# Routing order read out between the halves of the shared block, a gather in parts, and three weight loads that change places

## The reference

```python
def moe_ffn(h, w_router, router_bias, w_gate_up, w_down, shared_gate_up, shared_down):
    xf = h.reshape(-1, D)
    scores = jax.nn.sigmoid(xf @ w_router)
    sel = scores + router_bias
    grp = sel.reshape(N, N_GROUPS, N_EXPERTS // N_GROUPS)
    gscore = jnp.sum(lax.top_k(grp, 2)[0], axis=-1)
    _, gidx = lax.top_k(gscore, TOPK_GROUPS)
    ...
    _, idx = lax.top_k(jnp.where(emask, sel, -jnp.inf), TOP_K)
    w = jnp.take_along_axis(scores, idx, axis=1)
    w = w / jnp.sum(w, axis=-1, keepdims=True) * ROUTED_SCALE
    routed = routed_experts(xf, idx, w, w_gate_up, w_down)
    shared = swiglu(xf, shared_gate_up, shared_down)
    return routed + shared

def swiglu(x, w_gu, w_dn):
    g, u = jnp.split(x @ w_gu, 2, axis=-1)
    return (jax.nn.silu(g) * u) @ w_dn
```

## Time and profile before

| | us |
|---|---|
| median of 3 runs | 1260.34 |
| lowest, highest | 1259.62, 1261.03 |
| the profiled execution | 1259.55 |
| its span in the trace | 1257.70 |
| PE busy | 1081.1 (86%) |
| DVE busy | 505.1 (40%) |
| ACT busy | 248.6 (20%) |
| HBM read | 500.04 MB, 398 GB/s over the span |

### The profile page before, as it was taken

One profiled execution on the slowest core, in us unless ns is written; L12 is line 12 of the kernel. 1 busy time (PEld: TensorE's weight loads), 2 busy tenths in 40 slices (PEclk: granted clock), 3 DMA queues, 4 the chain that ended last, 5 costly groups with the idle time before them and its releaser, 6 DMA issues.

```text
span 1257.7 us, 16869 instructions
## 1 busy us (share of the span) xinstructions
PE 1081.1 (86%) x6524; PEld 599.6 (48%) x6524; DVE 505.1 (40%) x1131; ACT 248.6 (20%) x575; POOL 0.4 (0%) x5
## 2 busy tenths in 40 slices
PE   8999999998787868687879999999778687968786
PEld 6887586544333334343326678655333333424332
DVE  3597975432313132223236887542322313222322
ACT  1031722111101010101023472221100101110101
POOL 0000000000000000000000000000000000000000
PEclk9999999998889888899899999999988988989998
DMA  9999998999999999999999927899999999999996
GB/s 346 393 410 412 407 364 361 414 424 430 425 427 429 425 424 429 423 428 426 424 415 397 405 99 276 355 411 422 429 426 427 427 427 425 430 423 429 424 424 280
DMA packets 86327, 502.22 MB, mean 399 GB/s; under 512 B 9545, under 2 KB 34022, under 8 KB 43494
## 3 DMA queue, kind: packets, MB, share of 16 engines
q1 hardware_dynamic: 85782, 500.91, 97.0%
q10 hardware_dynamic: 464, 0.20, 0.1%
HBM read 500.04 MB, written 1.05 MB: 398 GB/s over the span
## 4 chain that ended last, share of the span: by engine, by line
PE 48%; DMA 39%; DVE 6%; SPq 5%; issue 2%; ACT 0%; DVEq 0%
PE bank L810 40%; DMA w_gu<-in_moe_w_gate_up 24%; DMA xn_hT<-in_moe_w_gate_up 10%; PE bank L813 2%; SPq L628 2%; DMA w_dn<-in_moe_w_gate_up 2%; PE bank L1087 2%; DMA w_gu_x<-in_ada_w 2%; SPq L635 1%; PE bank L1296 1%; PE bank L937 1%; PE bank L1135 1%; DMA ring<-in_ada_w 1%; DVE ada_row L2084 1%; DVE s_sb L1841 1%
## 5 line engine op out<-in xcount | busy, mean ns | idle before, releaser
L810 PE MATMUL bank<-w_gu,ring 128*32 128x512 f32 (+1 forms) x1408 | 350.3, 661 | 109.5 <-DMA xn_hT<-in_moe_w_gate_up 57.0
L810 PEld LDWEIGHTS bank<-w_gu,ring 128*32 128x32 f32 (+1 forms) x1408 | 97.3, 130 | 294.0 <-issue 293.5
L1995 DVE TENSOR_TENSOR hh<-sg,bank 128x256 f32<-128x256 f32 x44 | 27.3, 621 | 402.1 <-ACT sg L1581 402.1
L810 PE MATMUL bank<-w_gu_x,ring 128*32 128x512 f32 (+1 forms) x320 | 162.4, 664 | 9.7 <-DMA w_gu<-in_moe_w_gate_up 9.7
L810 PE MATMUL bank<-xn_hT,ring 128*32 128x512 f32 (+1 forms) x304 | 129.4, 586 | 17.8 <-DMA w_gu<-in_moe_w_gate_up 17.8
L810 PE MATMUL bank<-w_dn,ring 128*32 128x512 f32 x208 | 106.8, 733 | 14.8 <-DMA w_gu<-in_moe_w_gate_up 14.8
L1581 ACT ACTIVATE sg<-bank 128x256 f32<-128x256 f32 x44 | 16.9, 384 | 483.4 <-PE bank L810 483.4
L2012 DVE SCALAR_TENSOR_TENSOR bank<-bank,w_slot,gate 128x512 f32<-128x512 f32 x88 | 66.6, 759 | 89.3 <-PE bank L810 89.1
L810 PE MATMUL bank<-sel,h_hi 128*128 128x256 f32 x352 | 87.8, 290 | 0.0
L810 PE MATMUL bank<-sel,h_lo 128*128 128x256 f32 x352 | 84.2, 279 | 0.0
L1461 ACT ACTIVATE y_hi<-bank 128x512 fp32r<-128x512 f32 x88 | 52.6, 597 | 153.9 <-DVE bank L2012 153.7
(11 more groups left out here) (311 smaller groups left out, 1487.1 us busy)
## 6 DMA issues: line engine op xcount, KB each, us to landing
w_gu<-in_moe_w_gate_up SPq DMA_DIRECT2D x56, 2048.0 KB, 24.6
w_gu<-in_moe_w_gate_up SPq DMA_DIRECT2D x48, 1024.0 KB, 12.7
ring<-in_moe_w_down SPq DMA_DIRECT2D x44, 1024.0 KB, 29.2
ring<-in_ada_w SPq DMA_DIRECT2D x36, 1024.0 KB, 11.4
w_gu_x<-in_moe_w_gate_up SPq DMA_DIRECT2D x16, 2048.0 KB, 26.1
w_gu<-in_moe_w_down SPq DMA_DIRECT2D x24, 1024.0 KB, 22.1
xn_hT<-in_moe_w_gate_up SPq DMA_DIRECT2D x10, 2048.0 KB, 30.9
w_dn<-in_moe_w_down SPq DMA_DIRECT2D x18, 1024.0 KB, 28.5
```

What stands on the lines that cost most here:

```text
L810: return nc.tensor.matmul(o, a, b, start=first, stop=last)
L1995: v.tensor_tensor(hh[:, :].rearrange("s (f p) -> s p f", f=FE // P), sg[:, :].rearrange("s (p f) -> s p f", f=FE // P), bank[b][:, FE:2 * ...
```

## The change

Four things change, in both layers alike.

1. *Order.* DVE computes only the first `h_lo` piece, then `slot_of`, the keys and `hot`, then `select(0)`. The PE does the `hot` matmul in the middle of the second shared block, into bank 5 in place of bank 1. DVE casts the result into `tab_i` at once, and then does the other three `h_lo` pieces, the flags and the weights. The PE waits for `order` ahead of pass 0's gate/up.
2. *First gather.* `first_gather` takes the place of two calls of `gather_half`: in each half of the width first all `h_hi` products, then `h_lo` of the first token half, then of the second, with a wait for two and for four `h_lo` pieces.
3. *Tiles.* A unit 19 is added: the second gathered tile's ring slot. Expert 0's second gate/up half moves from unit 0 to unit 19, and from the early to the late list, second in it. It waits until the last chunk of the adaLN matrix in that slot is read.
4. *Shared down* moves from the list of pass 5 (unit 7) into the early list, at expert 0's former place, unit 0. After expert 0's half unit 19 isn't used for weights again. `assign_units` gives out the other units anew by its rule, which is not changed.

```diff
-EARLY_UNITS = ((("dn", 2, 0), 8), (("gu", 1, 0), 9), (("gu", 0, 1), 0), (("gu", 1, 1), 1), (("gu", 2, 0), 2), (("gu", 3, 0), 3),
+EARLY_UNITS = ((("dn", 2, 0), 8), (("gu", 1, 0), 9), (("dn", "shared", 0), 0), (("gu", 1, 1), 1), (("gu", 2, 0), 2), (("gu", 3, 0), 3),
                (("dn", 0, 0), 10), (("dn", 1, 0), 11))
-LATE_UNITS = ((("gu", 0, 0), 18), (("gu", 2, 1), 4), (("gu", 3, 1), 5), (("gu", 4, 0), 6), (("gu", 4, 1), 7))
+LATE_UNITS = ((("gu", 0, 0), 18), (("gu", 0, 1), 19), (("gu", 2, 1), 4), (("gu", 3, 1), 5), (("gu", 4, 0), 6), (("gu", 4, 1), 7))
...
-        loads.append([item for item in weight_items(p) if item not in unit] + ([SHARED] if p == SHARED_DOWN - 1 else []))
+        loads.append([item for item in weight_items(p) if item not in unit])
...
+                    elif v == GATHER_UNIT:
+                        freed(sp, ("ada", ADA_IN_WO[l], KT - 1))
...
-                shared_gate_up(0, 1, 6)
+                shared_gate_up(0, 1, 6, range(KT // 2))
+                pe.wait_ge(sem("hot"), l + 1)
+                mm(bank[5][0:1, 2 * E:3 * E], const("row")[0:E, :], hot[:, :], True, True).then_inc(sem("tables_ps"), 1)
+                shared_gate_up(0, 1, 6, range(KT // 2, KT))
...
+                def first_gather(half, banks):
+
+                    for h, ti, low in ((h_hi, 0, 0), (h_hi, 1, 0), (h_lo, 0, 2), (h_lo, 1, 4)):
+                        if half == 0 and h is h_lo:
+                            pe.wait_ge(sem("h_dve"), 4 * l + low)
+                        for kk in range(4):
+                            last = nc.tensor.matmul(bank[banks[kk // 2]][:, (kk % 2) * N:(kk % 2 + 1) * N], h[:, ti, 4 * half + kk, :],
+                                                    sel[:, ti, :], start=h is h_hi and ti == 0 and kk % 2 == 0, stop=h is h_lo and ti == 1,
+                                                    skip_group_check=True)
+                    last.then_inc(sem(f"gath_done{l}"), 1)
...
-                pe.wait_ge(sem("h_dve"), 4 * l + 4)
-                gather_half(0, 0)
-                gather_half(0, 1, (2, 3))
-                pe.wait_ge(sem("tables_sb"), 3 * l + FLAGS_SB)
-                mm(bank[1][0:1, 0:E], const("row")[0:E, :], hot[:, :], True, True).then_inc(sem("tables_ps"), 1)
+                pe.wait_ge(sem(f"sel_ready{l}"), 1)
+                first_gather(0, (4, 7))
+                first_gather(1, (2, 3))
+                pe.wait_ge(sem("order"), l + 1)
                 gate_up(0)
...
-                pe.wait_ge(sem("order"), l + 1)
+                pe.wait_ge(sem("tables_sb"), 3 * l + FLAGS_SB)
...
-                select(0)
-
-
                 dve.wait_ge(sem("ranks"), 2 * l + 2)
...
-                v.tensor_scalar(hot[:, :], const("rank_of", E), rank[:, 0:1], None, ALU.is_equal)
+                v.tensor_scalar(hot[:, :], const("rank_of", E), rank[:, 0:1], None, ALU.is_equal).then_inc(sem("hot"), 1)
+                select(0)
+                dve.wait_ge(sem("tables_ps"), 5 * l + ORDER_PS)
+                v.tensor_copy(tab_i[:, 0:E], bank[5][0:1, 2 * E:3 * E]).then_inc(sem("order"), 1)
+                for j in range(1, 4):
+                    low_rows(j)
```

More of the change, by code:

```diff
@@ L112, in weight_items @@
     return [("gu", j, half) for half in range(2) for j in js] + [("dn", j, 0) for j in js]
-EARLY_UNITS = ((("dn", 2, 0), 8), (("gu", 1, 0), 9), (("gu", 0, 1), 0), (("gu", 1, 1), 1), (("gu", 2, 0), 2), (("gu", 3, 0), 3),
+EARLY_UNITS = ((("dn", 2, 0), 8), (("gu", 1, 0), 9), (("dn", "shared", 0), 0), (("gu", 1, 1), 1), (("gu", 2, 0), 2), (("gu", 3, 0), 3),
                (("dn", 0, 0), 10), (("dn", 1, 0), 11))
-LATE_UNITS = ((("gu", 0, 0), 18), (("gu", 2, 1), 4), (("gu", 3, 1), 5), (("gu", 4, 0), 6), (("gu", 4, 1), 7))
+LATE_UNITS = ((("gu", 0, 0), 18), (("gu", 0, 1), 19), (("gu", 2, 1), 4), (("gu", 3, 1), 5), (("gu", 4, 0), 6), (("gu", 4, 1), 7))
 LAST_UNITS = ((("dn", 3, 0), 12), (("dn", 4, 0), 14))
-UNITS = 19
+UNITS = 20
+GATHER_UNIT = 19
 ROWS_UNIT, RING_UNIT = 18, 17
@@ L161, in assign_units @@
     signals = {u: [item] for item, u in unit.items()}
-    free = {u: turn_read(item) for item, u in unit.items() if u != ROWS_UNIT}
+    free = {u: turn_read(item) for item, u in unit.items() if u not in (ROWS_UNIT, GATHER_UNIT)}
     free.update({SECOND_UNIT: turn_of["shared_up"], HT_UNIT: turn_of["shared_up"], ROUTER_UNIT: -1, RING_UNIT: -1})
@@ L493, in build @@
                            + [xn_hT[:, 0, :], xn_hT[:, 1, :], ring[:, a, :], ring[:, b, :],
-                              gate_all[:, 0:2, :].rearrange("p a d -> p (a d)"), ring[:, free[0], :], w_gu_y[:, :]])
+                              gate_all[:, 0:2, :].rearrange("p a d -> p (a d)"), ring[:, free[0], :], w_gu_y[:, :], ring[:, free[2], :]])
             xg.append([ring[:, r, :].rearrange("p (k c) -> p k c", k=KT) for r in free[1:]])
@@ L1018, in experts, with shared_gate_up @@
                     last.then_inc(sem("h_ps"), 1)
-                def shared_gate_up(j, f, b):
+                def shared_gate_up(j, f, b, ks=range(KT)):
                     w = use(("sgu", l, j))
-                    for k in range(KT):
+                    for k in ks:
                         last = mm(bank[b][:, f * N:(f + 1) * N], w[:, k, f * P:(f + 1) * P], hT[:, k, :], k == 0, k == KT - 1)
-                    if f == FE // P - 1:
+                    if f == FE // P - 1 and ks[-1] == KT - 1:
                         used(("sgu", l, j), last)
@@ L1900, in experts, with low_rows @@
                 v.tensor_tensor(chosen[:, :, :], left[:, :, 0:E], choice[:, :, 0:E], ALU.not_equal).then_inc(sem("chosen"), 1)
-                for j in range(4):
+                def low_rows(j):
                     dve.wait_ge(sem("h_act"), 4 * l + j + 1)
@@ L1904, in experts @@
                         .then_inc(sem("h_dve"), 1)
+                low_rows(0)
                 dve.wait_ge(sem("ranks"), 2 * l + 1)
@@ L1969, in experts @@
                 last.then_inc(sem("w_of"), 1)
-                dve.wait_ge(sem("tables_ps"), 5 * l + ORDER_PS)
-                v.tensor_copy(tab_i[:, 0:E], bank[1][0:1, 0:E]).then_inc(sem("order"), 1)
                 dve.wait_ge(sem("tables_ps"), 5 * l + TABT_PS)
```

## The result

| | before | changed |
|---|---|---|
| median, us | 1260.03 (22 runs) | 1261.95 (22 runs) |
| lowest, highest | 1259.31, 1261.41 | 1259.09, 1263.82 |
| ratio, 95% interval | | 1.0015, 1.0009 to 1.0021 |
| the profiled execution, its span | 1259.55, 1257.7 | 1260.92, 1259.1 |

The change costs 1.9 us, where 0.2 was forecast. That is within the 0.2% that the prediction calls no change, yet the interval excludes zero.

What follows compares the result with a forecast made beforehand. A PE chain sets the time from 197 to about 241 us, then the DMA rate. PE chain 0.1 us per layer, 0.2 in sum, restart and later landings 0: 1260.34 + 0.2 = 1260.5 us, range 1257.0 to 1263.0.

Steps and rivals of the forecast that it cites:

- A: The hole moves from behind the routing to just before pass 2's release; 1260.5 us; chance 0.74 together with Rival D.
- rival C: PE really waits at hot in the shared block or at h_lo; 1263.1 us if DVE is 1.3 us slower; chance 0.11.
- Bytes at each release: Up to pass 2's first half both kernels release equal MiB; the 3.4 us head start becomes a hole before 241.5.
- Rival B: The routing hole closes for good: all 7.4 us come off, 1252.9 us; chance 0.08 in full, 0.07 in part.
- Routing order and first issue: Layer 0's routing: order at about 200.7 us, 5.5 us earlier; first routed transfer at 204.1, not 207.8.
- Rival D: SP is stuck at a wait ahead of the order, so no earlier order; time as A; chance 0.74 with A.
- The PE chain: PE work up to 240.5 us counts one to one; the new h_lo wait adds 0.1 us per layer, bounds 0 to 0.3.
- The restart: First 1 MiB issued into the dry queue at pass 2's release: 0 us taken, -0.6 to +0.1 per layer.
- What lands later: Expert transfers from the dip to shared down's old place land 2.46 us later; PE waits about 1.3 us; no cost.

Runs made afterwards that it cites:

- a_hold: Changed kernel with SP also waiting for the end of pass 0's first gate/up half before its first routed load; 1261.63 us.
- e_tiles: Kernel before with only the change's tiles (unit 19, expert 0's second half late, shared down early); +1.1 us against its runs of before.
- a_hold2: Changed kernel with SP also waiting for the first gathered tile's second half before its first routed load; between 1261.17 and 1261.46 us.
- a_gather: Changed kernel with the former first gather behind one wait for all four h_lo pieces; 2.1 us longer than the changed kernel.
- b_hold: Kernel before with SP also waiting for the end of pass 0's first gate/up half before its first routed load; 5.9 us more.
- b_short: Kernel before without the h_lo products (16 matmuls) in the gather for passes 2 and 3; -0.2 us, no difference.
- b_swap: Kernel before with pass 2's first half ahead of the order's later tables and the gather's second part; 0.2 us below its runs of before.

## Why the prediction was right, and where its sum was off

The forecast was no change and 1260.5 us, and the reason given for it, a hole that moves, is what the runs show. The size was not right: 1261.95 lies above A's own bounds (1259.3 to 1261.2) and is in the stated range only by what that range took in of rival C. Two terms of the sum were too small, the second with less proof.

**Bytes at each release: right, and the core of it.** Both kernels may have 28 MiB out at 234 and 31 at 240.6, so the head start of the routed loads turned into a hole in front of the release: 0.56 at 217:220, 0.77 at 240:242, by bytes 4.0 us where 3.4 were forecast. Rival B (1252.9) is out. `a_hold` is the direct proof: given back, the head start costs nothing. Rival B was also what the Trainium skill's page "Perfetto Trace Analysis", section "Optimization Strategy", would have one expect of closing the gaps of the most contended engine; in this case the gaps closed at the routing, opened again behind it, and nothing came of it.

**Routing order and first issue: right.** 200.49 for 200.7, first routed load 204.11 for 204.1. Rival D didn't occur.

**The PE chain: the step that was mis-sized.** I took 0.1 us per layer with bounds 0 to 0.3. It is 0.36 in layer 0 and 0.33 in layer 1 (43.91 against 43.58), outside the bounds, 0.7 us for 0.2. The `hot` matmul was booked as moved at no cost; matmul by matmul it costs 0.40 between the shared matmuls and gave back 0.20. The gather loses 0.15 at the wait for the last `h_lo`, too short to show in a list of waits. Only this 0.15 is rival C's mechanism, at about a ninth of its price (C wanted 1.3 us per layer).

**The restart: the second, as far as is known.** I took 0 out of -0.6 to +0.1 per layer, and the +0.1 had no row behind it. The first 1 MiB behind the dry queue landed after 6.2 us and 7.5 us, against 5.8 in the earlier trace rows, and `e_tiles`, with a restart and no longer chain, is 1.1 us over before (0.3 to 2.5 by its interval). What such a restart costs is open, since it isn't the same twice: behind the release at 240 and its counterpart in layer 1 the first 1 MiB took 5.8 and 5.7 us before, 7.2 and 5.7 in `e_tiles`, 7.5 and 5.1 in `a_hold2`.

The page "DMA: Bandwidth & Descriptors" of the Trainium skill, section "Anatomy of one DMA — SWDGE (gpsimd) path", gives 2.0 us plus bytes over 436 GB/s, 4.4 us for 1 MiB; a sum by it would have been 1257.7. The page gives it for transfers that GpSimd issues, which the prediction left out; all of these are issued by SP. Into a dry queue elsewhere 1 MiB took as little as 4.7 us (`a_gather`, issued at 219.35) and 5.0 (`b_hold`, at 211.14), near that figure; at the release at 240 no kernel was under 5.8, and the measurement decides.

**Put together.** In the two profiled executions the changed kernel is 1.4 us longer in span. Layer 0: its ranks matmul starts 0.28 earlier, its chain is 0.36 longer, so the release comes 0.08 later; the transfers lag 0.17 in the mean and 0.61 at the last engine. Layer 1's ranks matmul starts at 793.22 against 792.09, 1.13 later; its chain adds 0.33. That makes 1.46. Over the twelve other kernels the step from the lag at 328 us to that at 793 us scattered from -0.8 to +1.1 us, with none of the edits touching the work there. The completions say where it is made: in the full queue of layer 0's later passes. The last transfer of layer 0 that the changed kernel's chain of waits goes through landed at 643.04 against 641.96 before, 1.08 later, of which the mean of its completions is 0.15; the rest is its spread, 5.4 against 4.3. In nine of the thirteen kernels layer 1's ranks matmul lags by what the landings at 643 to 644 us lag, to 0.05 us. So in the traced execution most of layer 0's loss is the lag of one DMA engine, and only 0.15 us is lost by all 16. That 1.46 meets the 1.4 us of the span so well is in part luck: in between, at a landing of layer 1 (881.4 us before), the last engine was 2.6 us late.

**What lands later: right in kind.** Pass 4's last down was waited for 1.9 us (forecast 1.3), pass 5 began at 299.40 (298.8), pass 6's weights landed at 323.78 (323.2 plus the lag). The late five MiB were issued from 308.81 on, and the queue stayed full.

## What to carry to other kernels

Where transfers wait for buffers, count the bytes that may be out at each release before and after an edit; if they are equal, starting the transfers earlier only moves the hole. Test it cheaply with a hold: if holding the transfers back costs nothing, bringing them forward gains nothing. If it costs nearly its full length, the transfers are on a limit; if bringing them forward still gains nothing, as here, the releases are on one too, and neither alone is worth shortening (`b_short`). Read a hole by its GB/s as well as by its share. And price an instruction that moves within a saturated PE queue at both places, since the 0.35 us per layer that were lost here left no line in the list of waits.

## What the runs showed of the hardware

The 16 DMA engines fall apart and stay apart. In a full queue the spread of a transfer's completions doesn't shrink (2.4 to 2.6 us from 267 to 328 us in the changed kernel), so a lag of one engine is carried on until the queue next runs dry, and all that wait for a landing pay it. Over a whole layer it grows: before, from 1.5 us at 246 to 4.3 at 642. It grew at a restart: in `a_hold2` from 1.8 us to 3.2 us over the release at 241. But not only there. In `a_hold`, layer 1, it grew from 1.7 to 3.1 us, and a landing came 3.8 us behind the one ahead of it instead of 2.5, with the queue full:

```profile
845.00:850.00 5.00, 4.99 (x44) 3.10 (x48) 1.64 (x4) 1.09 (x2) 0.00 (x0) 1.00 1.01 416
...
q8 instruction: 1, 0.02, 1.2%
```

The second line is of the view of DMA queues for the same 5 us: one fetch of instructions of 16 KB, which took 1.0 us of one engine's time. In `b_hold` the same fetch, 2 us later, left the spread as it was (1.9).

In a full queue it is these fetches that move the engines apart. I took each landing between 252 and 630 us and between 850 and 1225 us in all 14 traces that was issued before its forerunner began to complete, and compared the two spreads. Where no fetch ran from 2 us before the forerunner's first completion up to the landing (1606 times), the spread grew by over 0.3 us once. Where one of 16 KB did (1182 times; 421 such fetches start in these stretches), it grew by over 0.3 us 79 times, by up to 1.7 us. So about every fifth fetch makes the last engine later; the others leave the spread nearly as it is.

At a dry restart the two are not separated: in 11 of the 14 kernels such a fetch starts between 240.6 and 242.9 us, close to the issue at the release. In `e_tiles` and `a_hold2` a single completion stands 2.2 and 1.5 us behind the 15th there, as a fetch would leave it, but the trace doesn't name the engines. Whether the fetches hit the same engines in every execution, so that they belong to a kernel, or by chance, is open too, for each kernel has one trace.

Nor does the spread at one place explain the cost: in `b_swap` it is 3.8 us at 328 us, after a fetch at 272.5, and the time is that of before. By 642 us before has spread to 4.3 itself and `b_swap` to 4.9, and its lag at the last engine is down from 1.03 to 0.20 us. What counts is how far back the last engine is where the layer ends.
